# Three feed-forward up projections of 256 tokens in seven block products, with the token halves as stationary operand

## What is computed

```python
def swiglu(h, w_in, w_out):
    gate, up = _split_last(h @ w_in, (D_FF, D_FF))
    return (jax.nn.silu(gate) * up) @ w_out

x = x + 0.5 * swiglu(rms_norm(x, ffn1_norm[l]), ffn1_w_in[l], ffn1_w_out[l])
...
x = x + 0.5 * swiglu(rms_norm(x, ffn2_norm[l]), ffn2_w_in[l], ffn2_w_out[l])
...
xl = xl + ml[5] * _swiglu(_modulate(_rmsnorm(xl, norm_g[l, 1]), ml[3], ml[4]), w_ffn_in[l], w_ffn_out[l])
```

## Time and profile before

| | us |
|---|---|
| median of the three runs (3288.01 to 3293.32) | 3292.65 |
| the profiled execution | 3296.3 |
| its span, first to last instruction | 3294.4 |
| TensorE busy in it | 3198.5 |
| VectorE / ScalarE / GpSimd busy | 1079.6 / 570.8 / 253.5 |

### The profile page before, as it was taken

The page is one execution under the profiler, slowest core; times in us unless marked ns, Lnnn a source line. Parts: engine busy times, 40 slices in busy tenths (PEclk is TensorE's granted clock), DMA queues, the critical chain, the costliest instruction groups (busy, mean ns, idle before and its releaser), DMA issues.

```text
span 3294.4 us, 41330 instructions
## 1 busy us (share of the span) xinstructions
PE 3198.5 (97%) x17812; PEld 2675.8 (81%) x17812; DVE 1079.6 (33%) x1887; ACT 570.8 (17%) x1127; POOL 253.5 (8%) x104
## 2 busy tenths in 40 slices
PE   8999999999999999999999999999999999899998
PEld 7888888788888865888478888888888788678887
DVE  1003732332012335423862344323323513721101
ACT  1003222130002112200530212111021211410100
POOL 0000000000001100122011111121210001000000
PEclk9999999899999999999999999999999999999999
DMA  5343542325433211233013242221222233133432
GB/s 205 140 157 136 196 181 79 128 77 219 153 131 138 103 52 51 80 153 100 26 52 141 77 160 96 103 77 59 108 102 77 77 137 119 52 141 128 150 132 101
DMA packets 33961, 378.39 MB, mean 115 GB/s; under 512 B 3328, under 2 KB 9600, under 8 KB 9856
## 3 DMA queue, kind: packets, MB, share of 16 engines
q1 hardware_dynamic: 29296, 370.68, 30.2%
q10 hardware_dynamic: 4496, 5.24, 0.7%
HBM read 370.67 MB, written 1.05 MB: 113 GB/s over the span
## 4 chain that ended last, share of the span: by engine, by line
PE 92%; DVE 4%; ACT 2%; issue 1%; DMA 0%; SPq 0%; DVEq 0%; ACTq 0%
PE bank L766 91%; DVE small L3014 1%; PE bank L769 1%; ACT arena L2149 0%; DVE arena L2741 0%; DVE h_T L2325 0%; ACT h_T L1735 0%; ACT arena L2160 0%; DVE arena L3024 0%; DMA masks<-first_consts_dram 0%; DVE arena L3058 0%; DVE small L3015 0%; DVE factors L2416 0%; DVE h_T L2308 0%; ACT arena L1767 0%
## 5 line engine op out<-in xcount | busy, mean ns | idle before, releaser
L766 PE MATMUL bank<-h_T,weights 128*128 128x256 f32 (+1 forms) x5296 | 1238.8, 391 | 25.6 <-ACT masks L1767 5.8
L766 PEld LDWEIGHTS bank<-h_T,weights 128*128 128x128 f32 x5296 | 1007.2, 192 | 222.9 <-issue 84.2
L766 PE MATMUL bank<-arena,weights 128*128 128x256 f32 x2840 | 625.7, 381 | 4.1 <-DVE arena L2819 2.5
L766 PEld LDWEIGHTS bank<-arena,weights 128*128 128x128 f32 x2840 | 540.8, 191 | 82.4 <-issue 5.2
L766 PE MATMUL bank<-factors,weights 128*128 128x256 f32 x1432 | 323.8, 380 | 1.9 <-DVE factors L2416 1.3
L766 PEld LDWEIGHTS bank<-factors,weights 128*128 128x128 f32 x1432 | 272.4, 190 | 39.0 <-issue 1.7
L2259 POOL TENSOR_TENSOR weights<-weights 128x1024 f32<-128x1024 f32 (+1 forms) x50 | 122.0, 2441 | 1803.2 <-DMA weights<-wide_slabs_dram 1704.3
L2433 DVE TENSOR_TENSOR arena<-bank,arena 128x512 f32<-128x512 f32 (+1 forms) x132 | 88.1, 667 | 406.8 <-PE bank L766 404.9
L1783 ACT ACTIVATE arena<-bank 128x512 f32<-128x512 f32 (+1 forms) x144 | 83.3, 579 | 691.8 <-PE bank L766 604.7
L766 PE MATMUL bank<-arena 64*64 64x64 f32 (+7 forms) x1592 | 185.6, 307 | 13.3 <-ACT arena L2160 9.0
L2264 POOL TENSOR_TENSOR factors<-weights 128x1024 f32<-128x1024 f32 (+1 forms) x50 | 132.2, 2643 | 722.0 <-PE bank L766 702.4
(11 more groups left out here) (300 smaller groups left out, 2285.5 us busy)
## 6 DMA issues: line engine op xcount, KB each, us to landing
weights<-wide_slabs_dram SPq DMA_DIRECT2D x151, 2048.0 KB, 7.8
weights<-down_slabs_dram SPq DMA_DIRECT2D x32, 1408.0 KB, 5.8
arena<-arena ACTq DMA_DIRECT2D x16, 256.0 KB, 10.0
masks<-second_consts_dram SPq DMA_DIRECT2D x1, 2176.0 KB, 8.7
masks<-second_consts_dram SPq DMA_DIRECT2D x2, 1024.0 KB, 6.8
x_T<-x_T_dram SPq DMA_DIRECT2D x1, 1024.0 KB, 5.8
x_T<-ctx_T_dram SPq DMA_DIRECT2D x1, 1024.0 KB, 11.3
out_dram<-h_T ACTq DMA_DIRECT2D x1, 1024.0 KB, 3.9
```

What stands on the lines that cost most here:

```text
L766: return mm(out, lhsT, rhs, start=start, stop=stop, skip_group_check=True)
```

## The change

The three stages `ffn1_up`, `ffn2_up` and `l1_ffn_up` (`HALF_STAGES`) are made in block products of their own, `HalfUnit`, one for a slab. Now the tokens are stationary and the weights move: the block rows of the output are the two token halves (128 each), the block columns the slab's 256 gate and 256 up columns. Each of the seven products is four matmuls of 128x128 stationary and 256 moving columns: 28 for a slab.

```diff
+            def half_product(key, name):
...
+                w, x = block_of(u, name), half_factor(u, name)
+                for k in range(4):
+                    if u.first and name in ("P1", "P2"):
+                        t.wait("h_ready")
+                    last = matmul(bank[u.bank[name]][:, 0:T], x[:, k], w[:, k * T:(k + 1) * T],
+                                  start=k == 0 and name in ("P1", "P2", "P5"), stop=k == 3)
+                last.then_inc(S["half_products"], 1)
...
+                for j in range(up.slabs + 1):
+                    for product in ("P1", "P3", "P2", "P7", "P5", "P6", "P4"):
+                        n = j - 1 if product in ("P3", "P7", "P4") else j
+                        if 0 <= n < up.slabs:
+                            half_product((up.name, n), product)
```

P3, P7 and P4 of a unit are made one unit late, between the products of the next. The accumulating bank (P1, P6, P7, P4) is 0, 3 and 4 in turn; P2 has bank 1, P5 and P3 share bank 2. The waits ahead of the products:

```diff
+                if name == "P1":
+                    arrived(u.st, u.j)
+                    if u.j >= 3:
+                        pe.wait_ge(S["dve_out"], UNIT[u.name, u.j - 3].hidden("A"))
+                before = (u.name, u.j - 1)
+                if name == "P2" and u.j:
+                    pe.wait_ge(S["half_joined"], HALF_JOIN["C11", before])
+                if name == "P5":
+                    if u.j:
+                        pe.wait_ge(S["half_joined"], HALF_JOIN["C12", before])
+                    pe.wait_ge(S["first_sums"], u.weights("S1"))
+                if name == "P6":
+                    pe.wait_ge(S["half_snapped"], u.snap("s1"))
+                    pe.wait_ge(S["first_sums"], u.weights("S2"))
+                if name == "P3":
+                    pe.wait_ge(S["half_snapped"], u.snap("s5"))
+                    pe.wait_ge(S["last_sums"], u.weights("S4"))
+                if name == "P7":
+                    pe.wait_ge(S["half_snapped"], u.snap("s2"))
+                    pe.wait_ge(S["last_sums"], u.weights("S3"))
+                if name == "P4":
+                    pe.wait_ge(S["half_joined"], HALF_JOIN["C22", key])
```

The output now has tokens on partitions, and the down projection wants features there. VectorE turns it in 32x32 pieces, and 16 transfers, which ScalarE begins, bring the pieces to their partitions. ScalarE's program of a stage:

```diff
+                def half_turn(u):
+                    act.wait_ge(S["turn_in"], u.half + 1)
+                    for i in range(4):
+                        to = A[:, u.j * 512 + i * P:u.j * 512 + (i + 1) * P]
+                        for j in range(4):
+                            src = half_turned(u)[32 * i:32 * i + 32, j * P:(j + 1) * P]
+                            act.dma_start(to[32 * j:32 * j + 32], src).then_inc(S[half_landed(u)[0]], 16)
+
+                units = [UNIT[st.name, j] for j in range(st.slabs)]
+                for j in range(st.slabs + 2):
+                    if j < st.slabs:
+                        half_snap(units[j], "s1")
+                    if 1 <= j <= st.slabs:
+                        half_gate(units[j - 1], "C12")
+                    if j >= 2:
+                        half_turn(units[j - 2])
+                    if j < st.slabs:
+                        half_gate(units[j], "C11")
+                        half_snap(units[j], "s5")
+                        half_snap(units[j], "s2")
```

`half_snap` copies P1, P5 or P6 out of PSUM (line 1876), `half_gate` applies Silu in place in SBUF (line 1881). VectorE's program:

```diff
+                    tt(c, c, up, mul).then_inc(S["dve_out"], 1)
+                    dve.wait_ge(S["dve_out"], u.hidden(which))
+                    if which == "B" and u.half >= 3:
+                        dve.wait_ge(S[f"hid_turned{u.half % 3}"], 256 * (u.half // 3))
+                    to = half_turned(u).rearrange("p (j c a t) -> p a c j t", j=4, c=2, a=2)[:, 0 if which == "A" else 1]
+                    return nc.vector.transpose(to, c.rearrange("p (c j t) -> p c j t", c=2, j=4))
+
+                for j in range(st.slabs + 1):
+                    u = units[j] if j < st.slabs else None
+                    last = units[j - 1] if j else None
+                    if u:
+                        block_sum((u.name, u.j), "S3")
+                    if last:
+                        half_join(last, "C12")
+                    if u:
+                        block_sum((u.name, u.j), "S4")
+                        half_join(u, "C11")
+                    if last:
+                        half_join(last, "C22")
+                        half_hid(last, "B")
+                        half_hid(last, "A").then_inc(S["turn_in"], 1)
```

The down projection keeps 22 matmuls for a tile, with the moving operand read as 2 x 4 pieces of 32 columns. Its first two tiles are made up to the hidden tiles of unit 8, and then their last four matmuls each, which need units 9 and 10:

```diff
+                        last = matmul(bank[b][:, 0:T].rearrange("p (a i t) -> p a i t", a=2, i=4), wtile(st, j, k), half_hidden(k),
+                                      start=k == 0, stop=k == FT - 1)
...
+                most, rest = range(FT - 4), range(FT - 4, FT)
+                for j in range(2):
+                    tile(j, most)
+                for j in range(2):
+                    tile(j, rest)
+                for j in range(2, KT):
+                    tile(j, range(FT))
```

More of the change, by code:

```diff
@@ L319, in taken, with __init__, weights, snap @@
         return "dve_out", self.st.dve0 + 4 * (self.j + 1)
+class HalfUnit:
+    narrow, down = True, False
+    def __init__(self, name, j, n, half):
+        self.name, self.j, self.n, self.half, self.st = name, j, n, half, ST[name]
+        self.x = (0, 3, 4)[j % 3]
+        self.bank = {"P1": self.x, "P6": self.x, "P7": self.x, "P4": self.x, "P2": 1, "P5": 2, "P3": 2}
+        self.first = j == 0
+    def weights(self, which):
+        return 2 * self.n + (1 if which in ("S1", "S3") else 2)
+    def snap(self, which):
+        return 3 * self.half + ("s1", "s5", "s2").index(which) + 1
+    def hidden(self, which):
+        return self.st.dve0 + 2 * self.j + (1 if which == "B" else 2)
 def make_units():
     units, runs, prod = {}, [], Marks()
+    products, joins = Marks(), Marks()
+    halves, wide = [], [0]
+    def half_run(name):
+        run = [(name, j) for j in range(ST[name].slabs)]
+        for key in run:
+            units[key] = HalfUnit(*key, len(units), len(halves))
+            halves.append(key)
+        for j in range(len(run) + 1):
+            for product in ("P1", "P3", "P2", "P7", "P5", "P6", "P4"):
+                n = j - 1 if product in ("P3", "P7", "P4") else j
+                if 0 <= n < len(run):
+                    products.add(product, run[n])
+            for which in ("C12", "C11", "C22"):
+                n = j if which == "C11" else j - 1
+                if 0 <= n < len(run):
+                    joins.add(which, run[n])
+    half_run("ffn1_up")
+    half_run("ffn2_up")
     for la, table in enumerate((WIDE_RUNS, NARROW_RUNS)):
@@ L567, in used_by, with made @@
             raise AssertionError
+        def made(key, product):
+            if UNIT[key].narrow:
+                return "half_products", HALF_PROD[product, key]
+            return "products", PROD[product, key]
         HALF_DOWN = DOWN // 2
@@ L595, in program, with half_hidden, half_place, half_turned @@
         HID_T1, HID_T2, HID_T4 = tiles(A, 11264, FT // 2, T), tiles(G, 0, FT // 2, T), tiles(F, 0, FT // 2, T)
+        def half_hidden(k):
+            part = A[:, (k // 2) * 512:(k // 2) * 512 + 512].rearrange("p (i c a t) -> p c a i t", i=4, c=2, a=2)
+            return part[:, k % 2]
+        def half_place(u, which):
+            base = FT * T + 768 * (u.j % 3) + 256 * ("C11", "C12", "C22").index(which)
+            return A[:, base:base + 256]
+        def half_turned(u):
+            base = FT * T + 3 * 768 + 512 * (u.j % 3)
+            return A[:, base:base + 512]
+        def half_landed(u):
+            return f"hid_turned{u.half % 3}", 256 * (u.half // 3 + 1)
+        def half_factor(u, product):
+            low, high, sums = factors(factor_set(u.name))
+            return {"P1": low[:, :, 0:P], "P2": high[:, :, 0:P], "P3": high[:, :, P:T],
+                    "P5": sums[0], "P6": sums[1], "P7": sums[2], "P4": sums[3]}[product]
         def factors(group):
+            if group in ("ffn1", "ffn2", "l1_ffn"):
+                h = H2[:, :, 0:T] if group == "l1_ffn" else H1
+                return h[:, 0:4], h[:, 4:8], [tiles(F, n * 512, 4, P) for n in range(4)]
             if group.endswith("_hid"):
@@ L2261, in _ @@
                 if before:
-                    pool.wait_ge(S["products"], PROD["P4" if u.first and u.down else "P6", before])
+                    name, count = made(before, "P4" if u.first and u.down else "P6")
+                    pool.wait_ge(S[name], count)
                     pool.wait_ge(S["last_sums"], UNIT[before].weights("S4"))
```

173 lines of the change are left out of this document (100 added, 73 removed).

## The result

The median of four runs is 3321.0 us (3312.7 to 3324.1), against 3293.0 (3288.0 to 3296.3) before. The ratio is 1.0082, with a 95% interval of 1.006 to 1.0105: the change makes the kernel **0.8% slower**, where 1.6% faster was forecast. The range given, 3235 to 3283, doesn't hold the time; the rival "issues pace the stage" does, with its 3302 to 3363. The profiled execution took 3324.1 us, span 3322.3.

What follows compares the result with a forecast made beforehand. The prediction took the up projections to be bound by TensorE alone: 57.0 us saved by fewer matmuls less 4.8 added on the path gives 52.2, from 3292.65 to 3240.5 us; range 3235 to 3283.

Steps and rivals of the forecast that it cites:

- issues pace the stage: Rival in the up stages: ScalarE's transfer issues at 0.62 to 0.74 us make TensorE wait, 3302 to 3363 us; chance 0.13.
- the price of an issue: ScalarE's queue, 16 transfers a unit: 0.42 us each, upper bound 0.74; at 0.42 TensorE does not wait.
- threshold of d = 0.52: Up stages: issue time d in us from which TensorE starts to wait for ScalarE's copy of P5.
- 3.8 + 16d: Time in us of the loop P3, join, Silu, transfers, Silu, copy at issue time d; passes 12.1 at d = 0.52.
- Decides from d = 0.60: Issue time in us from which the issues make the change slower; below it the change still wins.
- The products: Three up stages: 28 matmuls a slab for 32 save 19.0 us each, 57 us in all; 4.8 us are added back.
- The down projections: After the up stages: 176 matmuls kept, 76.1 us; moving operand in 32-column pieces costs nothing, bound 9%, 21 us in three stages.
- The transpose: VectorE, two of 128x256 a unit: taken as 0.5 us each, between 0.42 and some 1.7.
- Slabs: Weight slab ring: a successor must land within 12.1 us, lands in 7.6 to 9.0; margin 3 us or more, no cost.
- The open join: End of each up stage: the last unit's join of C22 has no other products to cover it, 0.8 us.
- Transfers one after the other: Rival: each transfer is paid to its landing before the next, 53 us a unit, some 4600 us; chance 0.01.
- the factor sums at the start of a stage: Four VectorE sums of 128x512 after the normalised tokens, 0.69 us each: 0 to 0.7 us added a stage, 0.3 taken.

Runs made afterwards that it cites:

- the runs with 12 and 14: The changed kernel with twelve or fourteen of a unit's sixteen transfers begun by ScalarE, the rest by SyncE: 3244.1 us with twelve, 3261.0 with fourteen.
- the kernel with the issues halved: The changed kernel with eight of a unit's sixteen transfers begun by ScalarE and the other eight by SyncE: 3242.2 us, ratio 0.9835 against the kernel before.

## Why the prediction was wrong

**The step that failed** is the price of an issue: "so I lay the price of those on their form and take 0.388 plus 0.03 gap, 0.42". Two neighbours were in the trace. The one that I took, 0.388, was a single transfer from SBUF to HBM. The one that I set aside, the four of L2124 with 0.59 to 0.94, was of the same queue, between SBUF and SBUF, and in a series. I explained its price by its eight runs, with the step between two transfers of SyncE as the proof. The runs show that the partitions and the bytes of a run don't carry it: 0.47 to 0.51 for the first, 0.61 to 0.62 at the median for each that follows, in every form tried. Eight runs for a partition were not tried. The four of L2124 take 0.60 us for the first and 0.70 for a following one at the median, so their eight runs may be worth some 0.09, but not the 0.23 that I gave them. The difference between 0.328 and 0.557 on SyncE has the sign of a series too, as the dearer one was issued 0.3 us behind the other, and their starts, 743.9 and 744.2, should have been read as well as their forms. But on that queue the step from a first issue to the next is 0.08 (0.507 to 0.591 with all issues on SyncE), so most of the 0.23 stays unexplained, and so does what lies between 0.388, towards HBM, and 0.47, within SBUF.

With the gaps and the long ones 16 issues came to 10.6 us at the median (10.1 to 11.9), 0.66 each, against 0.42 in the sum. The prediction's own threshold of d = 0.52, 8.3 us for sixteen, held nearly: the runs with 12 and 14 put it at 8.6 us.

**The rival's working**, 3.8 + 16d with a time of 3302 to 3363, was the right mechanism, and the time fell into it, but its parts were off in both directions. The loop is 3.4 and not 3.8 us beside the issues, since they start with the Silu and not behind it: the unit that begins at 60.22 lasts 14.3 us, where 3.8 + 10.95 would be 14.8. The last transfers delay a down projection by 2.2 us (6.7 in three), not 8.1. In the first stage the last 32 issues take 21.7 us, not 23.7, their end is 24.3 us behind the last P3 and not 26.6, the waiting matmul begins 1.2 later and not 3, and it was wanted at 22.7 and not at 21.5. And what it left out altogether is what a wait costs beside itself: the lower clock behind some of them, 18.7 us, and the restarts, 8.4 us, of the 80.7. "Decides from d = 0.60" would have been a little lower with them. On the line between its own 3302 (d = 0.62) and 3363 (0.74) the measured 0.66 to 0.67 lies at 3322 to 3327, and 3321 was measured; since these errors cancel, that it is so close is luck.

**The chances.** The rival had 0.13 for the reason that the four of L2124 are of this queue and both ends. That is the reason which was right; "eight times fewer runs" was hardly an argument against it.

**What held**, by the kernel with the issues halved:

- The products: 57.0 less 4.8 predicted, 52.2. The three pieces are 49.7 us shorter and the ratio of 0.9835 is 54 us of 3297. The forecast time, 3240.5, was that of this kernel (3242.2). The up stages take 136.6, 137.8 and 136.4 us, a little over the 134 to 136 named.
- The down projections: 76.1 predicted as before. In the kernel with halves they are 352 records in 76.14 us again, so a moving operand in pieces of 32 columns costs nothing, and the bound of 9% with its 21 us was not needed. In the changed kernel they are 80.7, 78.0 and 78.4, by the late transfers and, in the first, the clock behind the wait.
- The transpose: 0.45 us, taken as 0.5. GpSimd's sums 2.35 (2.38 and 2.60 in the earlier trace rows). But for the open join and the input sums at the start (both below), no stage waits for VectorE.
- Slabs: landing 7.9 us at the median, margin as predicted. The ring is no part of the loss.
- The open join: the wait is 0.62, 0.8 predicted.
- Transfers one after the other: excluded, 1.8 us to landing and sixteen in 11 us.

**Too small**: the factor sums at the start of a stage, 0.3 predicted. In the second stage the first of them is late by 1.6 us in the changed kernel and 1.85 in the one with halves, since it collides with GpSimd (below).

The Trainium skill ("DMA: Bandwidth & Descriptors", section "Issuing engines are not separate DMA queues") says that the time on the sequencer is usually small relative to the transfer. The prediction had weighed this against the row and given it no weight in the sum, rightly: here one issue is 0.61 us and its landing 1.8 at the median, a third. The last three issues of a series land later (about 6 us at the median), so a whole turn takes 16.5 us from its first issue to its last landing, and 10.6 of them are issuing. The other half of its statement is that beginning transfers on several engines saves the sequencer's time and nothing else. The runs agree that only issuing was saved, 79 us of it with two queues; but SyncE's queue alone gives 78, so it is the place of the issues that counts here and not that two sequencers share them.

## What to carry to other kernels

Take the price of a transfer's issue from a row of the same queue in a series, multiply it by the number of issues in a row, and ask what the next instruction behind them on that engine is and who waits for it: an issue is free until the queue's slack is used up (8.6 us here), and then each costs a wait in every turn of the loop. When the sum passes the slack, put the issues on a queue with nothing urgent in it, or in small groups between the instructions that others wait for; moving the whole series within the same queue only changed who waits. A kernel with the new products and the issues on SyncE or on both queues is 1.6 to 1.7% faster than the kernel before, and by these ratios 2.5% faster than the changed one.

## What the runs showed of the hardware beyond that

ScalarE's queue goes ahead while the engine works: series of issues start 0.01 us after the activation ahead of them (60.22 and 60.22, 68.86 and 68.85), but an activation behind them waits for all of them (10.9 us).

A short wait costs TensorE more than itself. Behind 2.32 us of waiting the granted clock of the unit was 0.88 and sixteen records took 5.41 us; behind 1.60 it was 1.00 and they took 3.72. Of the 28 waits for the copies in the changed kernel ten, of 1.97 to 3.05 us, were followed by slow records. The length of a wait doesn't decide it alone, since four of 2.25 to 3.42 us were not, among them these:

```profile
143.35 3.72 PE L850 MATMUL bank<-weights,h_T 128*128 128x256 f32 x16 [2.43 <-ACT arena L1876]
...
170.97 1.99 PE L850 MATMUL bank<-weights,h_T 128*128 128x256 f32 x8 [3.42 <-ACT arena L1876]
```

VectorE's sums with both operands in SBUF stretch when they begin beside one of GpSimd's. Timeline of the kernel after, start of the second stage:

```profile
803.81 2.34 POOL L2405 TENSOR_TENSOR weights<-weights 128x1024 f32<-128x1024 f32 x1 [8.99 <-DMA weights<-wide_slabs_dram]
...
804.53 2.17 DVE L2595 TENSOR_TENSOR factors<-h_T 128x512 f32<-128x512 f32 x1
...
806.74 0.69 DVE L2595 TENSOR_TENSOR factors<-h_T,factors 128x512 f32<-128x512 f32 x1
...
806.85 1.97 PE L850 MATMUL bank<-weights,factors 128*128 128x256 f32 x8 [1.60 <-DVE factors L2595]
```

A sum of the same size takes 2.17 us when it begins within GpSimd's sum, and ends 0.55 after that (806.70 against 806.15), and 0.69 once GpSimd is idle. The Trainium skill ("SBUF — State Buffer", section "SBUF: two separate sides") has it that a VectorE instruction with two SBUF inputs and a GpSimd one that reads SBUF exclude each other for the whole instruction. The trace agrees in this, with 1.5 us lost here. No run was made to undo this one.
